# Column widths of 264, 260 or 268, another order in the first and last stage, and the samples' products ahead of key-value, in a float32 decoder step on Trainium2

## The reference

```python
def retention_chunk(q, k, v, s_prev, log_gamma):
    scores = jnp.einsum('bhnd,bhmd->bhnm', q, k) * decay_mask[None].astype(q.dtype)
    inner = jnp.einsum('bhnm,bhme->bhne', scores, v)
    cross = jnp.einsum('bhnd,bhde->bhne', q, s_prev.astype(q.dtype)) * cross_decay[...]
    kv = jnp.einsum('bhmd,bhme->bhde', k * k_decay[...], v)
    return inner + cross, jnp.exp(log_gamma * L)[...] * s_prev + kv

def conv_ffn(h, ffn_state, w_in, conv_w, conv_b, w_down):
    up, gate = jnp.split(h @ w_in, 2, axis=-1)
    ext = jnp.concatenate([ffn_state.astype(up.dtype), up], axis=1)
    a = dwconv_valid(ext, conv_w) + conv_b
    return (jax.nn.silu(a) * gate) @ w_down, ext[:, -(FFN_CONV_WIDTH - 1):]
```

## Time and profile before

| | us |
|---|---|
| median of 3 runs | 1484.23 |
| lowest and highest | 1482.62, 1485.35 |
| the profiled execution, its own time | 1482.45 |
| its span in the profile | 1480.3 |
| TensorE busy | 1472.7 (99%) |
| VectorE busy | 777.9 (53%) |
| ScalarE busy | 520.6 (35%) |
| DMA | 171.91 MB, mean 116 GB/s |

### The profile page before, as it was taken

How to read it: one execution, slowest core, us unless ns; L and a number is a source line. 1 busy time by engine, 2 the same in 40 slices (tenths; PEclk the granted TensorE clock), 3 DMA queues, 4 the chain that set the end, 5 groups by cost and what they waited for, 6 DMA issues and landing times.

```text
span 1480.3 us, 27526 instructions
## 1 busy us (share of the span) xinstructions
PE 1472.7 (99%) x11534; PEld 1408.6 (95%) x11534; DVE 777.9 (53%) x1047; ACT 520.6 (35%) x734; POOL 5.0 (0%) x26
## 2 busy tenths in 40 slices
PE   9999999999999999999999999999999999999998
PEld 8699879969978999999999999999999999999998
DVE  7675457348446965555552325445465555554222
ACT  5352164155136543333331323222343333333222
POOL 0000000000000000000000000000000000000000
PEclk9999999999999999999999999999999999999999
DMA  6644343362454232222222322222322222222321
GB/s 240 221 164 151 135 193 123 144 226 101 150 188 183 92 101 85 99 85 85 95 93 86 100 86 86 98 89 87 98 89 86 90 95 85 98 86 91 98 86 58
DMA packets 47744, 171.91 MB, mean 116 GB/s; under 512 B 5609, under 2 KB 6249, under 8 KB 46625
## 3 DMA queue, kind: packets, MB, share of 16 engines
q1 hardware_dynamic: 47200, 170.45, 33.2%
q10 hardware_dynamic: 432, 0.27, 0.1%
q0 software_dynamic: 32, 0.03, 0.0%
HBM read 149.39 MB, written 21.55 MB: 115 GB/s over the span
## 4 chain that ended last, share of the span: by engine, by line
issue 77%; PE 22%; DMA 0%; DVE 0%; ACT 0%; POOLq 0%; POOL 0%; ACTq 0%; DVEq 0%
PE ps L404 11%; PE ps L511 5%; PE ps L551 1%; PE ps L592 1%; PE ps L588 1%; PE ps L569 1%; PE ps L585 1%; PE ps L541 1%; PE ps L491 0%; PE ps L437 0%; DMA mix_gain<-in_mix_gain_dram 0%; PE ps L525 0%; PE ps L599 0%; PE ps L557 0%; DVE h_lo L1160 0%
## 5 line engine op out<-in xcount | busy, mean ns | idle before, releaser
L844 ACT ACTIVATE w_hi<-w_raw 128x1024 fp32r<-128x1024 f32 x227 | 239.7, 1059 | 762.0 <-PE ps L404 477.9
L404 PE MATMUL ps<-h_hi,w_hi 128*128 128x264 f32 (+4 forms) x2304 | 470.4, 285 | 1.4 <-DVE h_lo L1160 1.4
L1132 DVE TENSOR_TENSOR w_lo<-w_raw,w_hi 128x1024 fp32r<-128x1024 f32 x227 | 276.7, 1222 | 365.9 <-ACT w_hi L844 365.7
L404 PE MATMUL ps<-h_lo,w_hi 128*128 128x264 f32 (+4 forms) x2304 | 468.1, 284 | 0.0
L404 PE MATMUL ps<-h_hi,w_lo 128*128 128x264 f32 (+4 forms) x2304 | 467.8, 284 | 0.0
L404 PEld LDWEIGHTS ps<-h_hi,w_hi 128*128 128x128 f32 x2304 | 357.9, 189 | 2.3 <-issue 1.7
L404 PEld LDWEIGHTS ps<-h_hi,w_lo 128*128 128x128 f32 x2304 | 357.7, 189 | 0.0
L404 PEld LDWEIGHTS ps<-h_lo,w_hi 128*128 128x128 f32 x2304 | 357.0, 189 | 0.0
L691 PE MATMUL ps<-z_hi,w_lo 128*128 128x264 f32 (+1 forms) x704 | 144.7, 283 | 0.0
L691 PE MATMUL ps<-z_lo,w_hi 128*128 128x264 f32 (+1 forms) x704 | 144.6, 283 | 0.0
L691 PE MATMUL ps<-z_hi,w_hi 128*128 128x264 f32 (+1 forms) x704 | 144.6, 283 | 0.0
(11 more groups left out here) (194 smaller groups left out, 1377.2 us busy)
## 6 DMA issues: line engine op xcount, KB each, us to landing
w_raw<-in_w_units_dram SPq DMA_DIRECT2D x227, 512.0 KB, 3.3
states<-in_state_ret_dram SPq DMA_DIRECT2D x32, 512.0 KB, 6.2
out_ret_s_dram<-states SPq DMA_DIRECT2D x32, 512.0 KB, 2.6
v_bcast<-v_scratch SPq DMA_DIRECT2D x8, 1024.0 KB, 5.7
x_res<-in_x_all_dram SPq DMA_DIRECT2D x8, 268.0 KB, 5.4
out_ret_p_dram<-tmp SPq DMA_DIRECT2D x4, 512.0 KB, 3.8
out_y_prompt_dram<-y_rows SPq DMA_DIRECT2D x4, 512.0 KB, 2.9
decay<-in_decay_dram SPq DMA_DIRECT2D x4, 287.0 KB, 4.5
```

Source lines behind the costliest of these rows:

```text
L404: out = mm(PS[:, 2 * s + half, at:at + n_col], a, b[:, lo:lo + n_col], start=first and n == 0, stop=last and n == 2)
L844: fn(WH[:, c % NS, :], RAW[:, c % NR, :], ACT.Copy).then_inc(hi_ready, 1)
L1132: tt(WL[:, c % NS, :], RAW[:, c % NR, :], WH[:, c % NS, :].bitcast(F32), ALU.subtract).then_inc(lo_ready, 1)
```

## The change

Widths: `C_RET` goes from 10 to 8 and FFN 0's up product starts at 8 (264 and 264 columns); FFN 0's gate stays at 12. All three input products and the output product of the short convolution start at 12 (264 and 260), FFN 1's up product at 12 (264 and 260), its gate at 16 as before. The convolution inside the FFNs reads its input two columns further in, so its output has the width of before. Queries are made from column 8 on (264 and 264), keys for all columns; scores, inner products and ScalarE's copies of them leave out the first 8 columns.

First stage: the two parts of the first weight unit go from ScalarE's to SP's queue, ahead of x tiles 0 and 1; x tile 0 is rounded, subtracted and multiplied in two parts of columns; 13 instead of 10 products of a constant go ahead. Heads: the samples' products move ahead of key-value, `outer(0)` ahead of the `KM` copies, `outer(1)` behind unit 11's split, `update(0)` ahead of unit 11's split on VectorE; the keys' tail goes to bank 3 instead of 1. Last stage: two transposes move ahead of sums of squares, and one eviction goes from VectorE to ScalarE.

The diff, cut to its core:

```diff
-C_RET = 10
-C_FFN = (10, 14)
+C_RET = 8
+X_HALVES = ((0, C_RET + N_RET // 2), (C_RET + N_RET // 2, N_RET // 2))
@@ SP @@
-            x_tile(0)
-            x_tile(1)
+            for n in range(2):
+                sp.dma_start(RAW[:, 0, 256 * n:256 * n + 256], w_all[0, :, 256 * n:256 * n + 256]).then_inc(part_in[n], 16)
+                x_tile(n)
@@ TensorE, first_qk @@
-                for _ in range(10):
+                for _ in range(13):
                     mm(PS[:, 7, 0:P], MEAN_D[:], MEAN_D[:], start=True, stop=True)
...
+                pe.wait_ge(part_lo, 1)
+                for half in range(2):
+                    pe.wait_ge(half_lo, half + 1)
+                    c = C_RET + half * (N_RET // 2)
+                    xh, xl = h_cols(HH, 0, c, N_RET // 2), h_cols(HL, 0, c, N_RET // 2)
...
@@ TensorE, head @@
-                    pair_of_k(0, PAIR_A, 0, T // 2, U_HEAD, h)
+                    pair_of_k(C_RET, PAIR_A, 0, N_RET // 2, U_HEAD, h)
...
+                        if j == 4 and e == 0:
+                            pe.wait_ge(v_some, 2 * h + 1)
+                        out = pe.transpose(PS[0:mn, (6, 6, 7, 7, 3)[j], at:at + P], K[:, e, m0:m0 + mn], IDENT[:])
...
+                        q0 = max(m0, C_RET)
+                        out = mm(PS[0:rows, bank, at + q0 - m0:at + m1 - m0], K[:, e, m0:m0 + rows], Q[:, e, q0:m1], start=e == 0, stop=e == 1)
...
+                pe.wait_ge(qm_ready, 3 * h + 3)
+                for b0 in (0, 4):
+                    for c in range(4):
+                        pe.wait_ge(s_in[b0 + c], 16 * h + 16)
...
+                out.then_inc(samp_done, 1)
 
                 pe.wait_ge(kn_ready, 4 * h + 4)
@@ TensorE, ffn @@
-                c0, n_in = C_FFN[l], T - C_FFN[l]
-                w, wo = n_in // 2, (n_in - 2) // 2
+                c0, n_in = (8, 528) if l == 0 else (12, 524)
+                w, wo = n_in // 2, (n_in - 4) // 2
...
-                    pair_of_k(c0 + 2, PAIR_B, u0 + 2, wo, 4, i)
+                    pair_of_k(c0 + 4, PAIR_B, u0 + 2, wo, 4, i)
@@ TensorE, final @@
                 y_rows(4, 1, range(4))
+                pe.wait_ge(fin_root, 1)
+                y_rows(6, 1, range(4, 8))
                 pe.wait_ge(fin_x, 7)
...
+                pe.wait_ge(fin_y, 8)
+                y_rows(3, 2, range(4, 8))
                 sample_squares(2, first=True)
@@ TensorE, short convolution @@
-                            pair_of_k(14 if which == 2 else 12, slots, U_SC_IN + n, w - 1 if which == 2 else w, 12, i)
+                            pair_of_k(12, slots, U_SC_IN + n, w, 12, i)
...
-                        out = three(slots[e], w - 1, lhs_pair(c, kk, e), ZH[:, k, 2:], ZL[:, k, 2:], k == 0, k == KD - 1)
+                        out = three(slots[e], w, lhs_pair(c, kk, e), ZH[:, k, :], ZL[:, k, :], k == 0, k == KD - 1)
@@ ScalarE @@
-            act.dma_start(RAW[:, 0, 0:256], w_all[0, :, 0:256]).then_inc(part_in[0], 16)
             act.dma_start(MIX[:], io["mix_gain"].rearrange("p k o -> p (k o)")).then_inc(mix_in, 16)
-            act.dma_start(RAW[:, 0, 256:512], w_all[0, :, 256:512]).then_inc(part_in[1], 16)
...
                 for n in range(5, 7):
                     split_hi(n + NS, U_HEAD, h)
+                outer(0)
                 for e in range(2):
                     act.wait_ge(mid_done, 2 * h + e + 1)
                     fn(KM[:, e * DV:(e + 1) * DV], PS[:, 6 + e, :], ACT.Copy).then_inc(mid_ready, 1)
                 split_hi(7 + NS, U_HEAD, h)
...
-                act.wait_ge(samp_done, h + 1)
+                outer(1)
+                act.wait_ge(kv_done, h + 1)
                 fn(OS[:], PS[:, 1, :], ACT.Copy).then_inc(os_ready, 1)
-                outer(0)
-                outer(1)
...
+            act.wait_ge(fin_t, 4)
+            fin_rows(1, 1, 6)
@@ VectorE @@
-                for n in range(5, 8):
-                    split_lo(NS + n, U_HEAD, h)
...
+                for n in range(5, 7):
+                    split_lo(NS + n, U_HEAD, h)
+                update(0)
+                split_lo(NS + 7, U_HEAD, h)
...
                 tt(KV, PS[:, 6:8, :].rearrange("p e v -> p (e v)"), KM, ALU.add).then_inc(kv_ready, 1)
-                for b in range(5):
+                for b in range(1, 5):
                     update(b)
...
             fin_rows(1, 0, 4)
-            fin_rows(1, 1, 6)
```

More of the change, by code:

```diff
@@ L1535, in sc_body @@
                     for t in range(2):
[L1536 to L1537 removed]
+                        a = halves(TMP[:, 2 + t, 0:N_SC])
+                        tt(a, a, slot(PAIRS[pair][t], w), ALU.mult).then_inc(sc_read, 1)
                     split_lo(U_SC_IN + NS + n0 + 5, 12, i)
```

165 lines of the change are left out of this document (82 added, 83 removed).

## The result

The kernel after takes 1473.38 us (median of 4 runs, 1473.21 to 1473.93) against 1484.26 for the kernel before beside it (4 runs, 1482.62 to 1485.35): a ratio of 0.9928 with an interval of 0.9911 to 0.9946, 10.9 us saved where 7.15 were forecast. The profiled executions are 9.0 us apart: 1482.45 and 1473.48, spans 1480.3 and 1471.4. The other 1.9 us lie in the runs of the kernel before, whose median is 1.8 above its profiled execution; experiments 6 and 7 are about them. Times inside an execution are counted from the start of its own span; the expectations of the experiments count some starts of other kernels from the start of before's, so their 31.39 for the end of after's first stage, for example, is 31.53 here.

What follows compares the result with a forecast made beforehand. TensorE, busy 99% in one unbroken matmul stream, was taken as the bound. Widths 5.95, dropped columns 0.15, samples' order 0, first stage 0.6 and last stage 0.45 sum to 7.15 us: 1484.23 to 1477.1, range 1473.0 to 1481.5.

Steps and rivals of the forecast that it cites:

- columns dropped in scores, inner: Heads: eight fewer columns in 6 score and inner-product matmuls a head save 38 ns each head, 0.15 us for four.
- order of the samples' products: Heads: samples' products moved ahead of key-value, taken at 0, bounds -0.1 (seams between kinds of matmuls) to +0.4 us.
- first stage: Start of kernel: first product at 6.3 to 6.7 us instead of 7.18; 0.6 us won, bounds 0.2 to 0.9.
- last stage: End of kernel: one eviction moved to ScalarE shortens VectorE's chain; 0.45 us won, bounds 0.1 and 0.7.
- a width that leaves 2 when divided by 4 costs some 3 ns more than its columns do: TensorE's matmul pairs: claimed from widths like 262 and 258; the change removes them, widths' sum 5.95 us.
- the rival: Matmul pairs: columns alone decide, the excess belongs to the place (first column, first product of a pass); 1484.2 us, chance 0.08.
- read another tile: Argument against that rival: `ret_z` and the convolution's output use another tile and rotate banks, yet stand above 242.1 ns.
- columns alone: Matmul pairs: 0.8 ns more for each of 2208 pairs growing by 2 columns, +1.8 us; time 1484.2 us, chance 0.08.
- the pair of 264 and 264: Width not in before's trace: taken as 243.9 ns, bounds 242.1 and 244.6, the upper near single 264s in the last stage.
- moved alone they cost nothing: Heads: the samples' same 32 records, 3.57 us in head 0, standing elsewhere in TensorE's order, change no time.
- The rival about V's broadcast: Heads: `outer(0)` holds ScalarE for V's broadcast, delaying `KM` copies and TensorE; slower, about 1488 us, chance 0.03.
- the price of a late tile is its lateness once: First stage: x tiles issued two DMAs, 0.9 us, later cost that once; 0.6 us won was still taken.

Runs made afterwards that it cites:

- experiments 6 and 7: 6: kernel before, unchanged, profiled again, 1485.24 us; 7: kernel before with 13 instead of 10 warm-up products, median 1482.54 us.
- o_old: Kernel after with the samples' products behind key-value again on all three engines, as before the change: median 1474.65 us, ratio 0.9939.
- w_narrow: Kernel after with both FFNs' up products at the old widths (264 and 262, 264 and 258) from first columns 8 and 12: 1473.4 us.
- w_start: Kernel after with both FFNs' up products read two columns further right (from 10 and 14) at the new widths: 1477.25 us.
- s_mix: Kernel after with all first-stage DMAs as before (part, gain, part on ScalarE's queue), halves and 13 warm-ups kept: median 1473.04 us, ratio 0.9928.
- f_queue: Kernel after with both parts of the first weight unit on ScalarE's queue behind the gain load, x tiles first on SP's: median 1473.05 us, ratio 0.9931.
- l_old: Kernel after with the last stage of before (one eviction back on VectorE, two transposes behind the squares): 1475.03 us, one run.
- b_warm13: Kernel before with 13 instead of 10 warm-up products, nothing else: median 1482.54 us over eleven runs, ratio 0.9993.

## Why the prediction was right, and where it wasn't

**The bound** was read rightly. TensorE's stream set the time before and after; every part of the gain is in starts lying closer together or in the two ends, and no other engine came up.

**The size by terms**, forecast, and measured in the two profiled executions. Of the queries' 0.72 the first head's 0.18 lies inside the first stage, whose own loss is then 0.75.

```
                                  forecast   measured
FFN 0 up                          1.4        1.66
heads' gates                      0.9        1.0
ret_z                             0.35       0.84
FFN 1 up                          1.7        1.63
short convolution in, out         1.0        1.16
queries                           0.6        0.72
columns dropped in scores, inner  0.15       0.35
order of the samples' products    0          1.3
first stage                       0.6       -0.75
last stage                        0.45       1.06
sum                               7.15       9.0
```

The order's 1.3 and the dropped columns' 0.35 are the 0.33 and 0.08 us a head between after, `o_old` and before, in four heads. The range held (1473.0 to 1481.5, measured 1473.38), but partly by luck: the order's 1.3, the landing's 0.6 and the 1.9 of the medians had no place in the sum, and only the first stage's loss, 1.35 below its term, took some of it back.

**Widths: right in sum, wrong in cause.** The failed step is "a width that leaves 2 when divided by 4 costs some 3 ns more than its columns do". `w_narrow` has the widths and costs 0.3 ns a pair; `w_start` has the first columns alone and costs 3.0 and 5.1. The forecast held because the change mends both at once, which the prediction had noted of the rival. Its argument against the rival, that `ret_z` and the convolution's output "read another tile", was the mistake: these too were read from columns that leave 2, `ret_z` in every second k tile, and `ZH` from column 2 on in tiles of 524. Of the rival's form the first column is right and the place in the pass wrong, as is "columns alone": an added column that fills a width up to 264 costs nothing (two of them save 0.3 ns a pair). The mis-sized term is the pair of 264 and 264: taken as 243.9 ns with bounds from 242.1 to 244.6, measured 242.6 (`ret_z`) to 243.4 (FFN 0, mean of ten passes). The row of single 264s at the last stage, 244.5 a pair, was the misleading neighbour.

Not settled: in FFN 1 the start alone costs 5.1 ns in `w_start`, but start and width together cost only 3.1 in before, so the effects don't add there; in FFN 0 they nearly do (3.0 and 0.3 against 3.1). And `w_start` moves the first column of both halves, so what each of them costs wasn't tried.

**The Trainium skill's formula** (same page, Back-to-back issue gap) gives N / 2.4 + 2.5 ns, 112.5 for 264 columns; the trace of after has 121.4, half of the 242.9 of FFN 0's pass above, and `w_start` 1.5 more from a start that leaves 2. The page also says that a sustained stream is paced by weight load and matmul together; the level may come from that, but no rule of it knows the moving operand's first column, and no run here took the weight loads apart.

**Order of the samples: the term taken at 0 was a gain of 1.3 us**, outside its bounds of 0.1 us gained to 0.4 lost. The failed step is "moved alone they cost nothing". The seams were named as the only possible gain and then sized with no row; starts across them (0.73, 0.52, 0.32) stood in before's timeline. The rival about V's broadcast didn't show: no wait on `KM` in after.

**First stage: the failed step is "the price of a late tile is its lateness once"**, set against an earlier start. The first product did start at 6.7, and the tiles behind it came 1.6 us later, which ate the start and 0.75 more. `s_mix` and `f_queue` show it: with the weights' two parts back on ScalarE's queue the same stage ends 0.65 and 0.56 us earlier. The prediction counted the two DMAs ahead of every x tile (0.9 us) and then took their cost as covered. What the three more warm-ups are worth was not seen at all: they were counted as a delay, while they take the longer runs away (experiment 7).

**Last stage:** the mechanism is right, and up to the issue of the last block so is the size, 0.45 us. The sum took the landing behind it as unchanged; it is 0.6 us shorter, and `l_old` gives both back.

**Traces and medians.** The forecast of 1477.1 was the sum on the median 1484.23. Of the 3.7 us by which it lies high, 1.8 are in the table; the other 1.9 are that most executions of the kernel before are 1.3 us or more longer than the one profiled. In the one such execution that was profiled, 1.7 of its 3.0 us are in the first stage with the low clock and 1.2 in the tail. `b_warm13` takes 1.7 us from the median of those four runs, 1.15 from that of fifteen. Only the spread of the runs shown (2.7 us) was there to warn of it, and the prediction used it as noise to both sides.

## What to carry to other kernels

Where TensorE's stream is the bound, let each moving operand of float32r start at a multiple of four columns, in every k tile: pad a tile's row length and start two columns earlier, since the two columns that fill up a width cost nothing here and a start off the four costs 3 to 6 ns a pair. Compare rows by where in its tile an operand begins, not only by width. A profile is one execution: where runs spread by more than their stages do, look at the granted clock behind the first idle time of TensorE, and warm up until the data are there. In a last stage look at when each output block is issued, not only the last: here the last one's landing was worth more than its issue.

## What the runs showed of the hardware

- The first column of the moving operand (float32r, 264 and 260 or 264 wide): multiples of 4 take 242 to 243.4 ns a pair, from column 14 it is 246.7, from column 13 248.8; 12 against 8 makes no difference.
- Kinds of matmul meet at a price, with no wait recorded: from key-value's last product 0.73 us to the samples' and 0.63 to the inner ones, and 0.52 from the samples' last to either.
- TensorE idle for 2.0 us behind 4 us of small products: granted clock 0.50 from 8.27 to 11.68 us, and 1.7 us lost in the stage; idle for 1.4 us in one execution and for 0.5 us in another: 1.00.
- A DMA of 4 KB at the head of ScalarE's queue landed at 3.0 to 3.3 us in the eight executions with after's first stage and at 3.9 in `f_queue`; behind a part of the weights it landed at 5.35 to 5.63. Two queues, one with the weights' parts and one with x, brought x tile 2 in at 6.9 to 7.4, one queue for both at 8.1 to 8.8.
- The last output block of 128 rows landed 3.4 us behind its issue where the two blocks ahead of it went out 2.2 and 1.3 us earlier, and 2.8 where they went out 3.4 and 1.4 us earlier.
